# Full-height value products for the 16 meta keys in the attention rounds of a two-layer decoder kernel

## What is computed

```python
q, k, v, qi, ki, wi = (pad(t) for t in (q, k, v, qi, ki, wi))
score = jnp.einsum('bqhs,bqh->bqs', jax.nn.relu(logits), wib.astype(jnp.float32))
score = jnp.where((key_pos[None, :] <= qpos[:, None])[None], score, -jnp.inf)
_, idx = lax.top_k(score, topk)
...
s = jnp.einsum('bqhd,bqkhd->bqhk', qb, k_sel) * (HEAD_DIM ** -0.5)
p = jax.nn.softmax(jnp.where(valid[:, :, None, :], s, -jnp.inf), axis=-1)
return jnp.einsum('bqhk,bqkhd->bqhd', p, v_sel)
```

## Time and profile before

| | us |
|---|---|
| median of three runs | 2719.63 |
| profiled execution, device time | 2723.08 |
| its span | 2721.3 |
| block of `project_v` | about 362 to 422 |
| attention rounds | about 446 to 690 |
| TensorE busy | 2463.3 (91%) |
| VectorE (DVE) busy | 1994.3 (73%) |
| ScalarE (ACT) busy | 1700.3 (62%) |
| GpSimd (POOL) busy | 642.2 (24%) |

### The profile page before, as it was taken

How to read it: one execution, slowest core, us unless ns; L and a number is a source line. 1 busy time by engine, 2 the same in 40 slices (tenths; PEclk the granted TensorE clock), 3 DMA queues, 4 the chain that set the end, 5 groups by cost and what they waited for, 6 DMA issues and landing times. The chain is left out here.

```text
span 2721.3 us, 37516 instructions
## 1 busy us (share of the span) xinstructions
PE 2463.3 (91%) x12571; PEld 2096.7 (77%) x12571; DVE 1994.3 (73%) x2325; ACT 1700.3 (62%) x1800; POOL 642.2 (24%) x484
## 2 busy tenths in 40 slices
PE   8789987998895999999999589997959999999993
PEld 8779966886584788888888479996848888888882
DVE  4677775668558888988898644344469888988895
ACT  2367845666214787778777446564127877778773
POOL 0104715644000212121221211211001212122223
PEclk9899998998896999999999789998969999999996
DMA  5502232321526879998799411104248789999994
GB/s 172 126 1 94 78 96 84 93 57 32 169 97 256 312 258 372 364 372 282 296 370 365 161 63 39 39 24 144 79 170 317 268 310 371 369 365 362 375 360 147
DMA packets 115273, 565.16 MB, mean 208 GB/s; under 512 B 23520, under 2 KB 27872, under 8 KB 65904
## 3 DMA queue, kind: packets, MB, share of 16 engines
q1 hardware_dynamic: 89776, 512.15, 51.5%
q0 software_dynamic: 25408, 51.84, 7.0%
HBM read 574.22 MB, written 74.34 MB: 238 GB/s over the span
## 5 line engine op out<-in xcount | busy, mean ns | idle before, releaser
L1967 DVE TENSOR_TENSOR e0wlo<-e0raw,e0whi 128x2048 fp32r<-128x2048 f32 x214 | 486.6, 2289 | 69.3 <-ACT e0whi L1815 69.2
L1967 DVE TENSOR_TENSOR e1wlo<-e1raw,e1whi 128x2048 fp32r<-128x2048 f32 x208 | 472.8, 2288 | 66.3 <-ACT e1whi L1815 66.3
L1815 ACT ACTIVATE e0whi<-e0raw 128x2048 fp32r<-128x2048 f32 x214 | 409.9, 1916 | 104.4 <-PE e0u L90 42.1
L1815 ACT ACTIVATE e1whi<-e1raw 128x2048 fp32r<-128x2048 f32 x208 | 398.3, 1916 | 101.4 <-PE e1u L90 42.2
L88 PE MATMUL odd_ps<-h2T_hi,odd_w_hi 128*128 128x348 f32 x480 | 171.2, 357 | 6.2 <-DVE odd_w_lo L2433 6.2
L89 PE MATMUL odd_ps<-h2T_lo,odd_w_hi 128*128 128x348 f32 x480 | 155.2, 323 | 0.0
L90 PE MATMUL odd_ps<-h2T_hi,odd_w_lo 128*128 128x348 f32 x480 | 154.9, 323 | 0.0
L88 PE MATMUL m_y<-m_whi,m_xhi 128*128 128x512 f32 (+1 forms) x304 | 121.5, 400 | 24.2 <-DVE m_wlo L1547 23.8
L90 PE MATMUL m_y<-m_whi,m_xlo 128*128 128x512 f32 (+1 forms) x304 | 119.7, 394 | 0.0
L89 PE MATMUL m_y<-m_wlo,m_xhi 128*128 128x512 f32 (+1 forms) x304 | 119.7, 394 | 0.0
L88 PE MATMUL e0g<-e0whi,e0xh 128*128 128x512 f32 x284 | 115.6, 407 | 1.7 <-DVE e0xl L1972 1.7
(11 more groups left out here) (456 smaller groups left out, 7057.7 us busy)
## 6 DMA issues: line engine op xcount, KB each, us to landing
e0raw<-in_moe_w_gate SPq DMA_DIRECT2D x72, 1024.0 KB
e0raw<-in_moe_w_up SPq DMA_DIRECT2D x72, 1024.0 KB
e0raw<-in_moe_w_down SPq DMA_DIRECT2D x72, 1024.0 KB
e1raw<-in_moe_w_gate SPq DMA_DIRECT2D x70, 1024.0 KB
e1raw<-in_moe_w_up SPq DMA_DIRECT2D x70, 1024.0 KB
e1raw<-in_moe_w_down SPq DMA_DIRECT2D x70, 1024.0 KB
qki_w_raw<-in_w_even SPq DMA_DIRECT2D x22, 512.0 KB, 5.1
odd_w_raw<-in_w_odd SPq DMA_DIRECT2D x20, 512.0 KB, 3.7
```

What stands on the lines that cost most here:

```text
L1815: act.activation(w_hi[:, i, :], raw[:, i, :], ACT.Copy).then_inc(hi_done[i], 1)
L1967: dve.tensor_tensor(w_lo[:, i, :], raw[:, i, :], w_hi[:, i, :].bitcast(F32), ALU.subtract).then_inc(lo_done[i], 1)
```

## The change

Five things are changed:
- POOL clears key block 0 of `v` at the start of `project_v`; ACT's first copy into `v` waits for that. Rows 16 to 127 of block 0 hold zeros then.
- DVE clears key block 0 of `pT` at the start of the rounds; ACT and TensorE wait for it (`padded` 3 for 2).
- `turned` transposes 128 columns of `pr` for key block 0 in the rounds of query blocks 1 to 8 (16 in those of block 0), and writes 128 rows. The added columns are probabilities of the first 112 tokens behind the meta keys.
- `values` multiplies all 128 rows for every key block, key block 0 and the rounds of query block 0 among them. The added rows meet zeros in `v`.
- The row counts in `p_high` and `p_low` are written with `key_rows`; they come out as before.

```diff
+            pool.memset(v[:, 0, :, :].bitcast(F32), 0.0).then_inc(v_zero, 1)
             for k in range(KC):
                 pool.wait_ge(hi_done, k + 1)
...
                 act.wait_ge(mm_done, b + 1)
+                if b == 0:
+                    act.wait_ge(v_zero, 1)
...
+        def key_rows(n):
+            return toks(STEPS[n][1])
...
                     for j in js:
-                        a = (j % GROUP) * P
-                        last = pe.transpose(t_ps[k % 2][0:toks(j), a:a + q], pr[0:q, n % 2, tok0(j):tok0(j) + toks(j)],
-                                            const[0:q, C_ID:C_ID + q])
+                        a, w = (j % GROUP) * P, key_rows(n)
+                        last = pe.transpose(t_ps[k % 2][0:w, a:a + q], pr[0:q, n % 2, tok0(j):tok0(j) + w], const[0:q, C_ID:C_ID + q])
...
-                    last = pe.matmul(out, v[0:toks(j), j, h, :], pT[0:toks(j), n % 2, j, :, 0:q], start=(j == 0), stop=(j == b))
+                    last = pe.matmul(out, v[:, j, h, :], pT[:, n % 2, j, :, 0:q], start=(j == 0), stop=(j == b))
...
-            pe.wait_ge(padded, 2)
+            pe.wait_ge(padded, 3)
...
-                    rows = META if len(js) == 1 and js[0] == 0 else P
+                    rows = key_rows(n)
...
             act.wait_ge(ready, 1)
+            act.wait_ge(padded, 3)
...
             dve.memset(den[:], 1.0)
+            dve.memset(pT[:, :, 0, :, :].bitcast(F32), 0.0).then_inc(padded, 1)
             for i in range(2):
                 ins = dve.memset(t_ps[i][:], 0.0)
```

More of the change, by code:

```diff
@@ L745, in project_v @@
         chain, glu_out, glu_in = c.sem("vs_chain"), c.sem("glu_out"), c.sem("glu_in")
-        thr_fixed, signed, z_done, mask_done, plain = (c.sem("vs_" + n) for n in ("thr_fixed", "signed", "z_done", "mask_done", "plain"))
+        thr_fixed, signed, z_done, mask_done, plain, v_zero = (
+            c.sem("vs_" + n) for n in ("thr_fixed", "signed", "z_done", "mask_done", "plain", "v_zero"))
         block = c.block()
```

## The result

The changed kernel takes 2704.47 us (median of 7 runs, 2701.52 to 2709.91) where the kernel before takes 2719.36 (median of 7 runs): a ratio of 0.9943, 95% interval 0.9932 to 0.9953, or 14.9 us less. In a later set of runs the same pair gave 0.9959 (0.9945 to 0.9972), 12.2 us between the medians. The forecast was 19.1 us less, 2700.5, with a range of 2691 to 2709: the first median lies inside the range, and 2709.85 of the later set just above its end.

The account below looks back on a forecast made before the run. TensorE's order was taken to set the pace up to 592.5 us, later shared with DVE and ACT. 14.9 + 2.0 + 1.2 + 1.3 - 0.3 = 19.1 us less made the median 2700.5 us, range 2691 to 2709.

Parts of the forecast that it names:

- the first stretch: Attention rounds before 592.5 us, convolution taps woven in: 14.9 us saved, 35 of 40 rounds saving the whole 0.385.
- the exit step: From the 16-row product to the next in one sum: 0.31 us, then 0.23, against a normal 0.12, no wait.
- The price of the turns: Transposing meta keys with 128 columns for 16: priced at 0, or 3.9 us cost if the wider weight loads were exposed.
- the memsets: POOL's clearing ahead of W_v's low parts costs 0.3 us (0 to 0.95); DVE's of `pT`, at the rounds' start, 0.
- The 0.385: TensorE's surplus in us at each place where a 16-row value product stands among 128-row ones, saved by 128 rows.
- the block-8 rounds behind a block-0 round: Four rounds whose product waits for DVE to empty the output bank: 0.30 us saved each, 1.2 us together.
- The third stretch: Rounds from 630 to 664.5 us: 2.6 us by count, half or less taken as TensorE idles 8.2 us; 1.2 us.
- the tail: Rounds from 664.5 to 690 us: 3.0 us by count, at most 1.5 because of SyncE's last load; 1.3 taken.
- Rival 1: The surplus belongs to beginning a sum, not to rows, and the wider turn load is exposed: 2723.8 us; chance 0.05.
- Rival 2: TensorE's gain is caught by other engines in half of the rounds, 14.9 becoming 7.5: 2711 us; chance 0.09.
- Rival 3: More TensorE idling from 592.5 us lowers the clock, sign under 0.77; at worst costs 41 us, 2741; chance 0.04.
- the sum of the bounds: Most the rounds could save with nothing caught: 16.6 us before 592.5 us, 23.3 us over all four stretches.

Follow-up runs that it names:

- e7_conv_first: Changed kernel with ACT's copy of a finished convolution group put ahead of the output's low part; 2705.38 us, 0.9939 of before.
- e9_changed_again: The changed kernel, nothing altered, run once more in a later set; 2709.85 us, 0.9959 of before.
- e1_products_only: Changed kernel with its products over 128 rows, but the meta keys turned with 16 columns as before; 2704.98 us, 0.9940 of before.
- e8_all_full: e7_conv_first with the turn of block 0 and the turned denominators over 128 rows and columns too; 2701.26 us, 0.9926 of before.
- e10_all_full_again: e8_all_full, nothing altered, run once more beside the changed kernel; 2701.07 us, 0.9919 of before.
- e4_two_apart: Kernel before with products of key blocks 0 and 2 over 16 rows, block 1 over 128; 2754.74 us, all 72 rounds 256.93 us.
- e5_rows_64: Changed kernel with the product of the meta keys over 64 rows instead of 128; rounds took 237.64 us.
- e2_turns_only: Changed kernel with its 128-column turns and both memsets, but the meta-key product over 16 rows as before; 2726.48 us beside 2722.12 before.
- e3_two_adjacent: Kernel before with the products of key blocks 0 and 1 both over 16 rows, side by side; rounds took 240.81 us.

## Why the prediction came out as it did

**The mechanism, right.** "The surplus is 0.09 + 0.19 + 0.11 = 0.39 us" for each low product: it vanished from the products, came back with 64, 32 and 16 rows, and was paid twice where there were two excursions. The total, 14.9 us for 19.1, is short by terms of the sum that were sized too large, the first stretch above all. The reading that settled it beforehand was the exit step inside one sum, with no wait between its products.

**The price of the turns, right at 0, and the memsets, slightly off.** POOL's memset took 0.95 us and its first piece started at 359.80, where it would have started about 0.7 us behind ACT's first at 358.91; but ACT's sign came 11.36 us after ACT's first piece, 11.29 before. It cost 0.07 us and not 0.3: POOL's first piece was 0.2 us late and the eight took 10.44 us in place of 10.55, and the block as a whole took the same time. DVE's memset of `pT` took 0.48 us ahead of a wait that shrank from 2.46 to 1.92 us: covered.

**The first stretch, 11.7 for 14.9.** The 0.385 holds. Up to round 41 the rounds of query blocks 2 to 7 without a new wait gain 0.38 to 0.41 us each; a round of block 1, which has only one product behind the low one, gains 0.28, and 0.10 of the step after it falls to the next round. What was mis-sized is what waits catch: the forecast let 35 rounds save the whole, and nine of these met a wait. (Round 43 gained only 0.06 us without one; why is open.) I had found one kind of place, the block-8 rounds behind a block-0 round, and it is there in all four: the product starts 0.15 us behind the end of DVE's L1316, with TensorE idle for 0.12 and 0.11 us in rounds 19 and 37 and not in the other two. The four pairs gained 0.25 to 0.56 us for the 0.30 forecast. Round 37: L1316 ends at 556.05 us and the product starts at 556.20. TensorE's and DVE's timeline of the changed kernel, rounds 36 and 37 (as the earlier trace rows):

```profile
554.19 0.26 PE L1151 MATMUL o_ps<-pT,v_hi_lo 128*128 128x32 f32 x1
554.29 0.37 PE L1129 MATMUL s_ps<-k_hi,q_hi_lo 128*128 128x272 f32 x1
...
555.62 0.43 DVE L1316 TENSOR_TENSOR oT<-o_ps,oT 64x256 f32<-64x256 f32 x1
...
556.20 0.59 PE L1151 MATMUL o_ps<-pT,v_hi_lo 128*128 128x256 f32 x3
```

Two others I had not looked for: `c_ps`, the one bank of the convolution, 2.1 us in seven places, and the turned denominators, 0.96 us where there was 0.19. Together 2.9 of the missing 3.2 us. The sign of it was in the trace of before, though no wait was recorded: ACT's copy (L1195) of the same group ended at 463.79 us and the tap that it releases started at 463.93, 0.14 us later. The taps that wait in the changed kernel start 0.14 to 0.15 us behind the copy too, so that is the time of the release itself and nothing of it was slack. Four of the seven taps already started 0.14 us behind the copy before the change, and their rounds gained -0.02 to 0.01 us; in the other three the distance was 0.18 to 0.20, and the rounds gained 0.10 to 0.11. The denominators stood 0.15 and 0.14 us behind DVE's split before, and 0.15 and 0.15 now. At these six places TensorE had been waiting before the change, with the matmul ahead of the wait still counted as busy. `e7_conv_first` shows the first of the two; for the second no kernel was run.

**The third stretch and the tail, 0.4 for 1.2 and 0.2 for 1.3.** Here the two profiles of the changed kernel differ. I had named the load of the convolved rows as what is late next in the tail, and expected SyncE's wait for the other engines behind it to shrink from 1.5 us to nearly nothing. The load and the store ahead of it moved with the rounds (the store, SyncE's L1025 and now L1032, from 667.22 to 649.93 us). SyncE's own waits at the end of the block, first in the changed kernel's profile and then in `e9_changed_again`:

```profile
SPq L1038 <- DMA glu<-conv_rows: 5.8, 1, 5.8
...
SPq L117 <- PEq L117: 2.2, 1, 2.2
```

```profile
SPq L1038 <- DMA glu<-conv_rows: 7.0, 1, 7.0
...
SPq L117 <- PEq L117: 0.2, 1, 0.2
```

In the first the other engines are last, in the second the load is, as forecast. What differs is the granted clock. From the last product of round 62 to the last `oT`, before, changed kernel, changed kernel again (PE, PEld, DVE, ACT, POOL, clock, DMA share, GB/s):

```profile
658.44:689.20 30.76, 25.68 (x120) 19.53 (x119) 23.52 (x50) 16.65 (x41) 5.10 (x6) 0.72 0.51 140
```

```profile
640.96:671.50 30.54, 23.42 (x121) 19.53 (x119) 23.58 (x51) 16.94 (x41) 5.27 (x6) 0.72 0.51 141
```

```profile
641.07:670.00 28.93, 21.12 (x120) 17.31 (x119) 23.14 (x50) 16.48 (x41) 4.95 (x6) 0.85 0.54 148
```

At 0.72, the clock of before, the tail gave 0.2 us; at 0.85 it gave 1.8, and counted from the last product of round 62 the next block began 1.4 us earlier than before, near the 1.3 forecast. `e1_products_only` and `e7_conv_first` (0.86 and 0.87) also end with SyncE waiting 0.2 us for the others, `e8_all_full` and `e10_all_full_again` (both 0.73) with 0.7 and 1.9. In the third stretch the clocks are 0.90, 0.85 and 0.92, and the gains 0.4 and 1.1 us for the 1.2 forecast. So the terms for these stretches were right for one execution and too large for the other. Why the clock comes out one way or the other is open.

At equal clock, DVE's splitting of the turned keys takes part of the gain. TensorE's timeline at the end of the rounds in the changed kernel:

```profile
663.53 0.74 PE L1140 MATMUL t_ps<-const,pr 128*128 128x128 f32 x5 [0.92 <-DVE pT L1304]
664.02 0.95 PE L1151 MATMUL o_ps<-pT,v_hi_lo 128*128 128x256 f32 x6
665.95 0.85 PE L1151 MATMUL o_ps<-pT,v_hi_lo 128*128 128x256 f32 x5 [0.97 <-DVE pT L1304]
```

The same two waits were 0.52 and 0.59 us before: each grew by what the product ahead of it saved. They are 0.92 and 0.97 us in `e9_changed_again` too, so they are not what sets the two profiles apart.

**The rivals.** Rival 1 is refuted by `e4_two_apart` and `e5_rows_64` (the price follows the rows) and by `e2_turns_only` (the wider load costs nothing). Rival 2, the gain caught by the others, is what happened to a fifth of the first stretch. Rival 3, the clock, did not undo the gain, but it is not nothing: 0.76 in the third stretch, just under the 0.77 that I had named as its sign, where there was 0.81, and it decides over some 2 us of the later stretches. In the sum of the bounds, 39 x 0.385 + 5 x 0.33 is 16.7 and not 16.6; nothing hangs on it.

## What to carry to other kernels

In a stream of full-height products on TensorE, one short contraction costs 0.39 us, three times a product of 256 columns: fill it up to 128 rows with zeros on one side and finite values on the other, or put all short ones side by side so that one excursion serves them. Find such places by the distance between starts, not by durations or idle time, since none of it is recorded as waiting. And before a saving on a busy engine is counted in full, ask for every buffer that the engine takes up again how early it came free: where that lead is smaller than the saving, only the lead is gained. Count the lead from the earliest start that the release allows, here 0.14 to 0.15 us behind the end of the work that releases; a start at just that distance is a wait already, recorded or not.

## What the hardware showed beyond that

- Each change of height costs 0.19 us, the way in and the way out alike: 0.09 on the step across it and 0.10 to 0.11 on the step behind. With two 16-row products side by side the surplus over a normal step is 0.09, 0.10, 0.09 and 0.10; with one, the second of the first pair and the first of the second fall together, 0.09, 0.19, 0.11. The sum is the same for 16, 32 and 64 rows.
- The weight loads show the change too. In the changed kernel the load for the product at 547.52 us starts at 547.40, one step ahead, under the tap. In the kernel before, the first 128-row product behind the 16-row one starts at 560.55 and so does its load:

```profile
547.40 0.19 PEld L1151 LDWEIGHTS o_ps<-pT,v_hi_lo 128*128 128x128 f32 x1
```

```profile
560.55 0.19 PEld L1145 LDWEIGHTS o_ps<-pT,v_hi_lo 128*128 128x128 f32 x1
```

  Up to round 44 of the kernel before, all 40 loads of the first product behind a 16-row one start within 2 ns of it, the loads of the 16-row products at most 0.03 us ahead of theirs, and all 140 between two products of 128 rows start 0.11 to 0.12 us ahead. In `e3_two_adjacent` the second of the two 16-row products has its load 0.11 to 0.12 us ahead again, so a load that doesn't go ahead comes with the change of height, and not with the low height.
- A weight load of 16 columns and one of 128 (88 and 149 ns in the earlier trace rows) made no difference to the rounds: 145.24 and 145.45 us with the wide and the narrow one.
